# Activation tiles of the later stages 128 bytes behind their first home instead of 192, and every buffer behind them 64 bytes lower

## What is computed

```python
def hybrid_layer(...):                       # first block, 2 layers; in layer 0 also for hc
    z = modulate(rms_norm(h, norm1_w), sh1, sc1) @ w_in
    ya = mla_mixer(...); yb = gla_mixer(...); yc = na_mixer(...)
    h = h + g1 * (ga * (ya @ w_a_o) + gb * (yb @ w_b_o) + gc * (yc @ w_c_o)) @ w_out
    h = h + g2 * swiglu(modulate(rms_norm(h, norm2_w), sh2, sc2), w_ffn_in, w_ffn_out)

for l in range(DEPTH):                       # second block, 2 layers
    x = layer_norm(ALPHA * x + 0.5 * swiglu_2(x, ffn1_w_in[l], ffn1_w_out[l]), ...)
    x = layer_norm(ALPHA * x + hybrid_mixer(x, ...), ...)
    x = layer_norm(ALPHA * x + 0.5 * swiglu_2(x, ffn2_w_in[l], ffn2_w_out[l]), ...)
```

## The kernel before

| tile | start in bytes | start modulo 256 | start modulo 128 |
|---|---|---|---|
| raw, whi, wlo, h, xh, xl | 16512, 41088, 65664, 90240, 106624, 123008 | 128 | 0 |
| xh_n, xl_n | 106816, 123200 | 64 | 64 |
| stat, sq, y, yl, qdh, qdl, kvh, kvl, yh, hidh, hidl | 151360 and up | 64 | 64 |

## Time and profile before

### The profile page before, as it was taken

One profiled execution on the slowest core, in us unless ns is written; L12 is line 12 of the kernel. 1 busy time (PEld: TensorE's weight loads), 2 busy tenths in 40 slices (PEclk: granted clock), 3 DMA queues, 4 the chain that ended last, 5 costly groups with the idle time before them and its releaser, 6 DMA issues. The chain is left out here.

```text
span 2988.1 us, 53119 instructions
## 1 busy us (share of the span) xinstructions
PE 2819.1 (94%) x20725; PEld 2490.9 (83%) x20725; DVE 1358.3 (45%) x2407; ACT 1222.0 (41%) x1796; POOL 1124.8 (38%) x457
## 2 busy tenths in 40 slices
PE   7999999999899999999999999999889999988998
PEld 5667777887699998676888899898779989977898
DVE  4453553333443433545445434434654353366434
ACT  3332133433344444422356444444444444445443
POOL 1002030132255554111325454454526555533553
PEclk9998999899999999999999999999999999999999
DMA  6562353233266665221436565464326646622563
GB/s 223 179 212 81 105 153 96 53 95 105 71 183 197 183 197 160 65 59 29 110 81 192 162 188 174 141 186 151 107 78 178 197 147 197 192 94 67 160 192 99
DMA packets 570661, 413.56 MB, mean 138 GB/s; under 512 B 36566, under 2 KB 548252, under 8 KB 570524
## 3 DMA queue, kind: packets, MB, share of 16 engines
q1 hardware_dynamic: 570524, 411.69, 46.4%
HBM read 410.58 MB, written 2.88 MB: 138 GB/s over the span
## 5 line engine op out<-in xcount | busy, mean ns | idle before, releaser
L576 POOL TENSOR_TENSOR wlo<-raw,whi 128x768 fp32r<-128x768 f32 (+2 forms) x353 | 1024.5, 2904 | 1622.8 <-ACT whi L567 1621.7
L599 PE MATMUL psum<-xh_n,whi 128*128 128x256 f32 (+1 forms) x3208 | 922.3, 287 | 38.8 <-DVE xl_n L2225 9.0
L600 PE MATMUL psum<-xl_n,whi 128*128 128x256 f32 (+1 forms) x3208 | 906.6, 283 | 0.0
L601 PE MATMUL psum<-xh_n,wlo 128*128 128x256 f32 (+1 forms) x3208 | 906.5, 283 | 0.0
L576 DVE TENSOR_TENSOR wlo<-raw,whi 128x1280 fp32r<-128x1280 f32 (+2 forms) x353 | 528.8, 1498 | 616.4 <-ACT whi L567 616.2
L567 ACT ACTIVATE whi<-raw 128x2048 fp32r<-128x2048 f32 (+2 forms) x353 | 643.7, 1824 | 339.6 <-PE psum L970 157.8
L599 PEld LDWEIGHTS psum<-xh_n,whi 128*128 128x128 f32 x3208 | 608.0, 190 | 77.1 <-issue 33.4
L601 PEld LDWEIGHTS psum<-xh_n,wlo 128*128 128x128 f32 x3208 | 608.3, 190 | 5.3
L600 PEld LDWEIGHTS psum<-xl_n,whi 128*128 128x128 f32 x3208 | 607.0, 189 | 4.5
L970 PE MATMUL psum<-hidh,wlo 128*128 128x256 f32 x1232 | 341.8, 277 | 0.0
L968 PE MATMUL psum<-hidh,whi 128*128 128x256 f32 x1232 | 341.8, 277 | 0.0
(11 more groups left out here) (344 smaller groups left out, 3871.6 us busy)
## 6 DMA issues: line engine op xcount, KB each, us to landing
raw<-in_ffn_w_in SPq DMA_DIRECT2D x176, 512.0 KB
raw<-in_w_in SPq DMA_DIRECT2D x136, 512.0 KB
raw<-in_w_ffn_in SPq DMA_DIRECT2D x132, 512.0 KB
raw<-in_w_mod SPq DMA_DIRECT2D x96, 512.0 KB
raw<-in_ffn_w_out SPq DMA_DIRECT2D x88, 512.0 KB
raw<-in_w_ffn_out SPq DMA_DIRECT2D x66, 512.0 KB
raw<-in_w_out SPq DMA_DIRECT2D x32, 512.0 KB
raw<-in_w_a_o SPq DMA_DIRECT2D x16, 256.0 KB
```

Of the source, the lines that this page charges most:

```text
L576: eng.tensor_tensor(wlo[slot][:, c0:c1], raw[raw_at[p0] % 3][:, c0:c1], whi[slot][:, c0:c1].bitcast(F32), ALU.subtract).then_inc(sem_, 1)
L599: pe.matmul(dst, sh, mh, start=start and n == 0, stop=False, skip_group_check=True)
L600: pe.matmul(dst, sh, ml, start=False, stop=False, skip_group_check=True)
L601: last = pe.matmul(dst, sl, mh, start=False, stop=n == len(pairs) - 1, skip_group_check=True)
```

## The change

The narrow pair starts 128 bytes behind the wide one instead of 192, and all that is allocated behind it is 64 bytes lower.

```diff
         x_place = place[0]
         wide = sb("xh", [P, KD, T], F32R), sb("xl", [P, KD, T], F32R)
-        narrow = (at(x_place + 192, "xh_n", [P, KD, T], F32R)[0], at(x_place + KD * T * 4 + 192, "xl_n", [P, KD, T], F32R)[0])
-        place[0] += 192
+        narrow = (at(x_place + 128, "xh_n", [P, KD, T], F32R)[0], at(x_place + KD * T * 4 + 128, "xl_n", [P, KD, T], F32R)[0])
+        place[0] += 128
         par = sb("par", [P, 2 * P + 48])
```

## The result

The changed kernel is slower: 3050.49 us median of four executions (3047.18 to 3058.96) against 2994.21 of before (four executions, 2986.24 to 3000.36). The ratio is 1.0203, with a 95% interval of 1.0178 to 1.0228: the change costs about 2%, and the interval leaves open whether a little more or less. The forecast was 2995, no measurable change.

The account below looks back on a forecast made before the run. The prediction took TensorE's own work, busy 94% of the span, as the bound. It summed 2989.9 + 0 - 1.5 + 0 = 2988.4, plus 7.0 for a median, to 2995.4 us; range 2973 to 3025, the likeliest case's own 2979 to 3008.

Parts of the forecast that it names:

- What bounds the kernel: Whole span: TensorE, busy 94%, sets the time; feed-forward matmuls exceed 106.7 ns by 6.6 or 11.0 ns each.
- Step (a): Feed-forward matmuls, 11088 in seven parts: pace likely set by chance at a part's start; 0, bounds -14 and +35 us.
- Step (b): 456 matmuls with 512-column moving operands behind the pair: yh's slower pace may go; -1.5 us, between -3 and +3.
- Step (c): Second block's projections on xh_n, some 1100 matmuls broken up by attention: 0, with 3 us either way.
- Step (d): VectorE, ScalarE and GpSimd operands: no address effect shows, engines idle about half of each feed-forward part; 0.
- The rule that I weighed: TensorE's reads: two independent ports that never wait, so placement cannot matter and the change is worth exactly 0.
- the third pace: Feed-forward parts: all matmuls run at the 120.0 ns seen in generic_t; 3050 us, chance 0.08.
- All slow: Feed-forward parts: all lock to 117.7 ns, moving tile 128 modulo 256 from the weights; 3024.9 us, chance 0.19.
- All quick: Feed-forward parts: all at 113.3 ns, as starts on multiples of 128 bytes never straddle; 2973 us, chance 0.21.

Follow-up runs that it names:

- the bursts with no other engine at work: Kernel cut to matmul bursts on constant data, moving slices and weights shifted by set bytes; bursts took 11.16, 11.57, 11.65 and 11.77 us.

## Why the prediction was wrong

**What bounds the kernel** was right: 94% busy TensorE, and the whole difference is in the distance between matmul starts. Counting matmuls in fixed stretches was the view that shows it, before and after.

**Step (a) failed, and it is the step that decided.** It said that one address shows both paces, that the pace therefore goes by how a run starts, and took 0. The first half is true: the second trace of the kernel before has other slow parts than the first. The conclusion does not follow. The distance fixes which paces are possible, 113.3 or 117.8 at 192, 118.7 or 120.0 at 128, and something that stays open chooses among these, not the same way each time (in a feed-forward part, 120.0 at 128 was seen only twice, both times in the changed kernel). Two paces at one address say nothing of the paces at another. The term was not 0 but +50 us, beyond the +35 that I gave as its bound: I had bounded it by the slower pace seen on the same distance.

**The support for it was misread.** I set generic_t in layer 0 beside generic_t in layer 1 as one address with two paces. They are two addresses: wide in layer 0, narrow in layer 1. Read rightly, the rows say that distance 0 runs at 120.0 and distance 64 (the stationary activations 192 ahead of the moving panel) at 117.9, and would have put the address beside chance. The trace's names had it right, and I explained them away.

**Step (b)** took -1.5 us from the step between xh and yh and named its two readings. The remainder modulo 128 was the wrong one; the distance was the right one, and at 128 it stays 233 ns. Its value was 0.

**Step (c)** was of the right kind, following (a), and mis-sized: not 1100 matmuls and 0, but some 3500 and about +8 us, since layer 1 belongs to it. **Step (d)** was right: VectorE busy 1358.3 and 1358.5 us, and its split into the narrow tile takes 480 ns after 479.

**The rule that I weighed**, the Trainium skill's "SBUF — State Buffer", section "Who interferes with whom", that TensorE has two independent read ports and never waits on anyone, stands in a section on waits between engines, and nothing here speaks against it there: the bursts with no other engine at work run at the same paces as the kernel. What I drew from it, that placement cannot matter, does not hold: the same bursts run between 113.3 and 120.0 ns by the distance between their two operands alone, so the two reads are not independent of where they lie.

**Among the rivals** the third pace named the sum, 3050 us, with a chance of 0.08 and outside my range. Its mechanism was half right: two parts run at the 120.0 ns that it named, five at 118.7, which no row of before showed, and the projections and the merge of layer 1 make up part of the difference, so the sum came out right partly by luck. "All slow" had the right reason, a distance that no long run of the trace had, and the wrong pace. "All quick" was wrong in its reason; a start on a multiple of 128 bytes buys nothing. That a tile's matmuls might be slow at a distance nobody had run was worth more than 0.27 together, for the only price list I had, 120.0 ns at distance 0, 117.9 at 64 and 113.3 or 117.7 at 192, already showed a different value at each.

## What to carry to other kernels

Where TensorE runs long rows of matmuls with a weight load each, count matmuls in fixed stretches and look for paces that differ between tiles. Then try the moving tiles at 0, 64, 128 and 192 bytes modulo 256 from the stationary ones; 192 was best for 256 columns here and 0 for 512, and the spread was 6% and 3%. Where one placement shows two paces, profile it twice before blaming or excusing the address.

## What the runs showed of the hardware

The distance between the moving and the stationary operand, modulo 256 bytes, sets the pace of float32r matmuls of 256 columns with a 128 x 128 weight load each, at full clock: 120.0 ns at 0, 117.8 at 64 (113.3 in one burst with the activations stationary), 118.7 (in the kernel also 120.0) at 128, 113.3 or 117.8 at 192. With 512 columns it is 226.7, 229, 232 to 233 and 233.3. Moving both operands by 64 bytes changes nothing (ratio 1.0024, 0.9996 to 1.0052). That the read of the moving tile and the load of the next weights get in each other's way is a guess at the reason: both are busy all the time in these stretches, but no run here shows them meeting. Whichever of its two paces a part at 192 starts with, it holds to its end some 180 us later, even across stretches at another distance; with the low weights 128 bytes from the high ones the slower pace was not seen in any of 14 parts and 13 bursts.
